# Delta stage: 16x16 diagonal blocks of a triangular inverse taken through DRAM to VectorE, decays from loaded rows, keys four steps ahead

## The chip, the cores and the metric

One core of a Trainium2 chip runs the whole program once. The metric is the device time of that execution in microseconds; the median of three runs stands for a kernel. All data is float32.

## The reference, cut to what matters

The model has two blocks of two layers each over 512 tokens (two streams of 256) of width 1024. The change lies in one mixer of the second block, a delta rule with 8 key heads, 16 value heads, head size 128, in both directions. For one chunk of 128 tokens, one value head, one direction:

```
g      = cumulative sum of the log decays over the chunk
A[i,j] = beta[i] * exp(g[i]-g[j]) * (k[i].k[j])      for j < i, else 0
N      = (I + A)^-1                                  unit triangular, 128 x 128
R      = v - exp(g) * (k @ S)                        S: state ahead of the chunk
new    = N @ R, scaled by beta
out    = exp(g) * (q @ S) + (q.k * exp(g[i]-g[j]), j <= i) @ new
S      = exp(g_last) * S + (k * exp(g_last-g)).T @ new
```

N, the inverse of a unit triangular matrix, is what the change computes in another way. A triangular inverse can be built by doubling: with the inverses of two neighbouring diagonal blocks of size s known, the block between them is minus one inverse times the block of A times the other. Seven levels (s = 1, 2, 4, ... 64) give a 128 x 128 inverse.

## The kernel before, in words

All engines run programs written out by hand, with semaphores between them; nothing is scheduled by a tool. The delta stage (pe_delta, act_delta, pool_delta, dve_delta, sp_delta) has 16 problems: problem x = 4 i + c is chunk c of the head group i, and it holds 4 value heads in both directions, which are interleaved (number 2n of a row is direction 0, 2n+1 direction 1) so that one inverse serves both. Problem s updates the state in step s, and the loops run over s from -2 to 15. In step s each engine works on three problems, in an order that the loop body writes out: the state, new values and output of problem s; levels 3 to 6 of the inverse of a = s+1; the decays, keys and levels 1 and 2 of n = s+2. Level 0 is done on VectorE in dve_first.

A level is the same chain each time. ScalarE copies blocks of the inverse (act_mixed, line 1841), TensorE turns them (pe_turn, line 1569), ScalarE copies the result out of PSUM (act_turned, line 1847). Meanwhile TensorE multiplies A by the inverse so far (pe_left, line 1560) and VectorE masks that (dve_left, line 2093). Then TensorE multiplies both (pe_right, line 1578), and VectorE subtracts the product from the inverse (dve_right, line 2101). All of these work on four heads, 128 x 512 numbers.

The decays of problem n come from GpSimd (pool_gates, line 1906), a product with a triangular matrix on TensorE (pe_decays, line 1521), one exponential (act_decays, line 1825) and a mask on GpSimd (pool_masks, line 1926). The keys are products on TensorE (lines 1538 and 1539), multiplied by beta and the decays in dve_keys (lines 2109, 2113, 2118) and turned (pe_turn_keys, line 1547). The state part is pe_state_keys (1589), dve_state_in (2142), pe_new_values (1616), act_tails (1856), act_new_values (1868), pe_queries (1628), pe_out (1639), pe_state_next (1647), dve_state_next (2168) and dve_out (2155).

SP, the queue of the weight stream, writes a small table of decays to DRAM once (line 1688), and in a step with c > 0 loads two rows of it into all partitions (line 1700); pool_queries (line 1937) multiplies them by the queries. Ahead of the stage the projections run (line 230, with the convolution on VectorE at line 1953), behind it the z products (line 230 again). A wait blocks everything that stands behind it on its engine.

## Time and profile before

| | us |
|---|---|
| runs | 3119.36, 3128.99, 3128.74 |
| median | 3128.74 |
| span of the profiled execution (first to last instruction) | 3124.0 |
| busy: TensorE, weight loads, VectorE, ScalarE, GpSimd | 2994.7, 2337.4, 1396.2, 714.2, 623.6 |
| delta stage: first decay product, first z product after it | 1539.83, 1999.40 |

The profile is of one execution; its own time is not listed beside the runs, so its span of 3124.0 us is set beside their median. PE is TensorE, PEld its weight loads, DVE VectorE, ACT ScalarE, POOL GpSimd, SP SyncE; a q behind a name is that engine's queue of instructions. The granted clock 1.00 is 2.4 GHz, 0.50 is 1.2 GHz.

### The profile page before, as it was taken

To read this page: it belongs to the slowest core of one execution; us is meant where nothing else is said; L and a number is where in the kernel's file an instruction comes from. 1 tells how busy PE (TensorE), PEld (TensorE's weight loads), DVE (VectorE), ACT (ScalarE), POOL (GpSimd) and SP (SyncE) were. 2 spreads that over 40 slices of the span, in tenths; PEclk is the share of its full clock that TensorE was granted. 3 is DMA by queue.
4 is the path that set the end of the run, shared out by engine and by line. 5 is a ranking of instruction groups with operands and counts; after the bars stand their busy time and mean duration, and the time that the engine had idled before them with its cause. 6 is when DMAs were issued, how large, how long until landed. Compare 5 with 4: busy or idle time off the path is not lost.

```text
span 3124.0 us, 39229 instructions
## 1 busy us (share of the span) xinstructions
PE 2994.7 (96%) x15545; PEld 2337.4 (75%) x15545; DVE 1396.2 (45%) x2271; ACT 714.2 (23%) x1336; POOL 623.6 (20%) x497
## 2 busy tenths in 40 slices
PE   7999999999999999999889999989999999999999
PEld 3565488887666888544488988878688887698888
DVE  2245478753244332455456666575454222223100
ACT  1134121100332330333244444321100001321100
POOL 1000145443000000000122322244355441020000
PEclk9999999999999999999999999999999999999999
DMA  7446222223436444433100000222122223111443
GB/s 295 173 158 243 94 82 94 81 95 104 133 128 227 164 148 148 188 135 148 62 8 13 16 15 15 82 80 81 68 90 86 84 92 125 69 41 54 148 148 108
DMA packets 51952, 337.66 MB, mean 108 GB/s; under 512 B 6448, under 2 KB 8112, under 8 KB 12752
## 3 DMA queue, kind: packets, MB, share of 16 engines
q1 hardware_dynamic: 47088, 323.05, 28.5%
q10 hardware_dynamic: 3120, 7.14, 0.6%
q0 software_dynamic: 1584, 5.21, 0.5%
q8 instruction: 116, 1.90, 0.2%
q14 instruction: 44, 0.36, 0.0%
HBM read 334.26 MB, written 1.11 MB: 107 GB/s over the span
## 4 chain that ended last, share of the span: by engine, by line
PE 82%; issue 10%; DVE 3%; ACT 2%; DVEq 1%; DMA 1%; POOL 0%; POOLq 0%; ACTq 0%; SPq 0%
PE psum L2694 28%; PE psum L230 21%; PE psum L355 3%; PE psum L1578 3%; PE psum L264 3%; PE psum L660 3%; PE psum L1560 3%; PE psum L2250 2%; PE psum L1569 1%; PE psum L490 1%; PE psum L517 1%; ACT h_sb L1045 1%; PE psum L1616 1%; PE psum L1521 1%; PE psum L1639 1%
## 5 line engine op out<-in xcount | busy, mean ns | idle before, releaser
L230 PE MATMUL psum<-h_sb,ring 128*128 128x256 f32 (+1 forms) x2400 | 728.6, 464 | 18.7 <-ACT h_sb L1045 18.7
L230 PEld LDWEIGHTS psum<-h_sb,ring 128*128 128x128 f32 x2400 | 456.2, 192 | 278.9 <-issue 223.5
L2694 PE MATMUL psum<-arena,ring 128*128 128x256 f32 x1688 | 383.2, 379 | 0.2 <-DVE arena L2757 0.2
L2694 PEld LDWEIGHTS psum<-arena,ring 128*128 128x128 f32 x1688 | 320.6, 190 | 44.2 <-DVE arena L2757 0.6
L2694 PE MATMUL psum<-arena,c 128*128 128x256 f32 x1080 | 249.0, 379 | 0.0
L230 PE MATMUL psum<-arena,ring 128*128 128x256 f32 x992 | 220.9, 386 | 9.4 <-DVE arena L1015 4.7
L2694 PEld LDWEIGHTS psum<-arena,c 128*128 128x128 f32 x1080 | 205.1, 190 | 29.7 <-issue 1.9
L1906 POOL TENSOR_TENSOR ring<-c,gates 128x512 f32<-128x512 f32 x32 | 32.6, 1041 | 950.9 <-PE psum L264 735.0
L230 PEld LDWEIGHTS psum<-arena,ring 128*128 128x128 f32 x992 | 192.5, 194 | 37.8 <-DVE arena L1015 5.1
L2694 PE MATMUL psum<-h_sb,ring 128*128 128x256 f32 x688 | 155.7, 379 | 8.6 <-DVE kst L2773 8.6
L2709 POOL TENSOR_TENSOR rows<-ring 128x512 f32<-128x512 f32 (+1 forms) x39 | 52.9, 1356 | 553.1 <-DVE arena L2737 334.7
L2723 ACT COPY kst<-psum 128x256 f32<-128x256 f32 x55 | 20.3, 369 | 612.9 <-PE psum L2694 583.9
L2694 PEld LDWEIGHTS psum<-h_sb,ring 128*128 128x128 f32 x688 | 130.5, 190 | 28.6 <-issue 11.1
L1953 DVE SCALAR_TENSOR_TENSOR arena<-psum,vec,arena 128x508 f32<-128x508 f32 (+1 forms) x128 | 95.6, 748 | 113.6 <-ACT arena L1712 106.1
L472 DVE SCALAR_TENSOR_TENSOR x_sb<-psum,mods,x_sb 128x256 f32<-128x256 f32 x48 | 22.5, 482 | 239.5 <-PE psum L230 190.0
L355 PE MATMUL psum<-ring,h_sb 128*128 128x256 f32 x512 | 117.5, 389 | 10.4 <-ACT h_sb L1045 10.4
L264 PE MATMUL psum<-ring,silu_w 128*32 128x256 f32 x1536 | 107.9, 410 | 18.4 <-DMA ring<-in_stream 11.6
L2711 POOL TENSOR_TENSOR ring<-ring 128x512 f32<-128x512 f32 (+1 forms) x79 | 122.3, 1548 | 14.6 <-issue 4.0
L355 PEld LDWEIGHTS psum<-ring,h_sb 128*128 128x128 f32 x512 | 97.4, 193 | 31.9 <-issue 11.7
L2713 POOL TENSOR_TENSOR c<-ring 128x512 f32<-128x512 f32 (+1 forms) x79 | 113.0, 1430 | 11.2
L1560 PE MATMUL psum<-ring 128*128 128x128 f32 x768 | 105.3, 278 | 7.3 <-DVE ring L2101 6.6
L264 PEld LDWEIGHTS psum<-ring,silu_w 128*32 128x32 f32 x1536 | 43.5, 115 | 89.8 <-issue 47.4
(321 smaller groups left out, 4388.7 us busy)
## 6 DMA issues: line engine op xcount, KB each, us to landing
ring<-in_stream SPq DMA_DIRECT2D x302, 1024.0 KB, 4.8
arena<-decays SPq DMA_DIRECT2D x24, 256.0 KB, 3.6
x_sb<-in_x ACTq DMA_DIRECT2D x1, 2048.0 KB, 19.1
arena<-in_rpb POOLq DMA_DIRECT2D x32, 64.0 KB, 8.1
arena<-in_c POOLq DMA_DIRECT2D x1, 1120.0 KB, 9.7
x_sb<-in_ctx ACTq DMA_DIRECT2D x1, 1024.0 KB, 10.0
c<-in_c ACTq DMA_DIRECT2D x1, 1024.0 KB, 4.9
out<-x_sb POOLq DMA_DIRECT2D x1, 1024.0 KB, 5.0
```

The lines of the kernel that those rows point to most:

```text
L230: ins = pe.matmul(out_ap, lhs(k), rhs(k), start=first and k == 0, stop=last and k == nk - 1)
L264: ins = pe.matmul(bank(7)[32 * j:32 * (j + 1), 0:256], silu[:, a // (2 * ADA_CHUNKS), k, ADA_ROWS - 2 - 2 * q:2 * ADA_ROWS - 2 - 2 * q], w ...
L355: ins = pe.matmul(bank(rho % 4)[:, tt * 256:(tt + 1) * 256], h[:, k, tok:tok + 128], w[:, slot, k, :], start=k == 0, stop=k == KT - 1)
L660: ins = pe.matmul(bank(rho % 4)[:, 0:tok], w[:, n % RING, k, rho % 2 * 128:(rho % 2 + 1) * 128], y[:, k, 0:tok], start=first and k == ks[0 ...
L1560: ins = pe.matmul(self.part(self.b["bank"](2 * p), n), self.part(self.M[p], n), self.mixed(self.DT[x % 3], level, 1, n), start=True, stop= ...
L1578: ins = pe.matmul(self.part(self.b["bank"](2 * p + 1), n), self.part(self.LT[p], n), self.part(self.Y[p], n), start=True, stop=True)
L1953: ins = dve.scalar_tensor_tensor(z[:, :, lo:hi], u[:, :, lo + shift:hi + shift], b["v"]("dn_conv", 1, 20 * j + 5 * q + 2 + shift), z[:, :, ...
L2250: ins = pe.matmul(bank(rho % 2)[:, tt * 256:(tt + 1) * 256], h[:, k, tok:tok + 128], w[:, (n0 + c) % RING, k, :], start=k == 0, stop=k == ...
L2694: ins = pe.matmul(dst, self.seven_weights(n, i, k, nk), self.seven_moving(x, sums, i, k, nk), start=first and j == 0 and k == 0, stop=last ...
L2709: pool.tensor_tensor(s3, a11, a21, ALU.subtract)
L2711: pool.tensor_tensor(a21, a21, a22, ALU.add)
L2713: pool.tensor_tensor(s2, a21, a11, ALU.subtract)
```

## The change

- Levels 0 to 3 are no longer doubled over 128 x 128 tiles. The matrix A (negated, so that dve_right adds) of each problem is written to DRAM in two lanes: as it stands and turned. From there the 16 x 16 blocks on the diagonal are loaded so that one partition holds one block (32 blocks a lane and problem, two problems in 128 partitions). VectorE inverts all of them at once in the free dimension: dve_inverse_fours, dve_inverse_eights, dve_inverse_last, in every even step for the two problems s+2 and s+3. The inverses go to DRAM and come back as rows (E), and GpSimd writes them as diagonal blocks into the inverse (pool_inverse). Levels 4, 5 and 6 stay as they were, for one problem at a time, with one set of buffers.
- The decays: rows of the cumulative sums are loaded into all partitions (sum_rows), GpSimd adds a mask of 0 and -1e30 (pool_bars), and ScalarE takes eight exponentials of 128 columns with the negated sum as bias (act_decays). The products with a triangular matrix, their gates and masks are gone.
- Keys and decays are made for n = s+4 instead of s+2; the loops begin at -4. The decay tiles have five buffers, A four.
- The order on all engines is written anew, and SP's program with it.

The core of the diff:

```diff
+BASE = 16
+LEVEL0 = 4
+LEV = LEVELS - LEVEL0
+LEAD = 4
+KEYS_PITCH = 128 // BASE * (BASE * 128 + BASE)
...
+        for hv in range(12, DN_HEADS):
+            self.pe_turn_v(pe, hv)
+        for s in range(-LEAD, DELTA_STEPS):
             if s == 0:
                 pe.wait_ge(T["v_copied"], DN_HEADS)
                 pe.wait_ge(S["mods_ready"], 5)
...
+            a, n = self.problem(s + 1), self.problem(s + LEAD)
             c = s % 4 if s >= 0 else None
...
             if c is not None and c > 0:
                 self.pe_state_keys(pe, s, 0)
             if a is not None:
...
+                self.pe_left(pe, a, 4)
             if c is not None and c > 0:
                 self.pe_state_keys(pe, s, 1)
             if a is not None:
...
+                self.pe_turn(pe, a, 4)
+            if c is not None:
+                self.pe_key_turn(pe, s)
             if n is not None:
                 self.pe_keys(pe, n, 0)
+            if a is not None:
+                self.pe_right(pe, a, 4)
             if c is not None:
...
+                self.pe_new_values(pe, s)
             if a is not None:
...
+                self.pe_left(pe, a, 5)
+            if c is not None and c > 0:
+                self.pe_queries(pe, s, 0)
+            if a is not None:
+                self.pe_turn(pe, a, 5)
+            if c is not None and c > 0:
+                self.pe_queries(pe, s, 1)
             if n is not None:
                 self.pe_keys(pe, n, 1)
             if a is not None:
...
+                self.pe_right(pe, a, 5)
             if c is not None:
...
+                self.pe_out(pe, s, 0)
             if a is not None:
...
+                self.pe_left(pe, a, 6)
+            if c is not None:
+                self.pe_out(pe, s, 1)
             if n is not None:
                 self.pe_turn_keys(pe, n)
...
             if a is not None:
                 self.pe_turn(pe, a, 6)
             if c is not None and c < 3:
                 self.pe_state_next(pe, s, 0)
             if a is not None:
                 self.pe_right(pe, a, 6)
...
             if c is not None and c < 3:
                 self.pe_state_next(pe, s, 1)
...
+        T = self.S2
+        rows, sums = self.b["decays"], self.b["gsums"]
+        keys_d, inv_d = self.b["keys_d"], self.b["inv_d"]
+        def row_of(dram, s, d):
+            i, c = divmod(s, 4)
+            at = 32 * ORDER[d][c] + 16 * d + 4 * i
+            return bass.AP(tensor=dram.tensor, offset=128 * at, ap=[[0, 128], [1, 512]])
+        def sum_rows(x):
+            for d in range(2):
+                sp.dma_start(self.AT[x % 5][d], row_of(sums, x, d)).then_inc(T[f"rows{x % 5}"], 16)
+        def keys_out(x, lane, tile):
+            dst = bass.AP(tensor=keys_d.tensor, offset=(2 * x + lane) * 4 * KEYS_PITCH,
+                          ap=[[128, 128], [KEYS_PITCH, 4], [1, 128]])
+            sp.dma_start(dst, self.heads(tile)).then_inc(T["keys_out"], 16)
+        def own_blocks(x, lane):
+            src = bass.AP(tensor=keys_d.tensor, offset=(2 * x + lane) * 4 * KEYS_PITCH,
+                          ap=[[BASE * 128 + BASE, 32], [128, BASE], [1, BASE]])
+            at = 64 * lane + 32 * (x % 2)
+            dst = self.inv[at:at + 32, :].rearrange("p (r i) -> p r i", r=BASE)
+            sp.dma_start(dst, src).then_inc(T["blocks"], 16)
         sp.wait_ge(T["decays_out"], 1)
...
+        sp.dma_start(rows, self.decay_rows).then_inc(T["decays_out"], 16)
+        sp.dma_start(sums, self.gsum_rows).then_inc(T["decays_out"], 16)
+        sp.wait_ge(T["decays_out"], 33)
         sp.wait_ge(T["qkv_ready"], QKV_CHUNKS // 2 + 1)
...
+        sp.wait_ge(self.b["S"]["products"], 2 * self.b["sched"]["2z"][0])
+        for x in range(5):
+            sum_rows(x)
+        for s in range(-LEAD, DELTA_STEPS):
+            n = self.problem(s + LEAD)
+            if s > 0:
+                for d in range(2):
                     sp.wait_ge(T[f"op{d}"], s)
...
+                if n is not None:
+                    sum_rows(n)
+                if s % 4 > 0:
+                    for d in range(2):
+                        sp.dma_start(self.QE[d], row_of(rows, s, d)).then_inc(T["qd"], 16)
+            m = self.batch(s)
+            if m is not None:
+                sp.wait_ge(T["inv"], m + 1)
+                for lane, tile in enumerate((self.inv, self.inv_turned)):
+                    dst = bass.AP(tensor=inv_d.tensor, offset=(128 * m + 32 * lane) * 256, ap=[[64 * 256, 2], [256, 32], [1, 256]])
+                    sp.dma_start(dst, tile[64 * lane:64 * lane + 64, :]).then_inc(T["inv_out"], 16)
+                sp.wait_ge(T["inv_out"], 32 * (m + 1))
+                for x in (2 * m, 2 * m + 1):
+                    if x > 1:
+                        sp.wait_ge(T["id"], x - 1)
+                    src = bass.AP(tensor=inv_d.tensor, offset=(128 * m + 64 * (x % 2)) * 256, ap=[[BASE, 128], [8 * 256, 8], [1, BASE]])
+                    if x % 2:
+                        sp.wait_ge(T["inv_in"], 16 * x)
+                    sp.dma_start(self.E[x % 2].rearrange("p (h i) -> p h i", h=8), src).then_inc(T["inv_in"], 16)
+            if n is not None:
+                sp.wait_ge(T["kr"], 2 * n + 2)
+                keys_out(n, 0, self.LTK)
+                sp.wait_ge(T["keys_out"], 32 * n + 16)
+                own_blocks(n, 0)
+                sp.wait_ge(T["mc"], n + 1)
+                keys_out(n, 1, self.M[n % 4])
+                sp.wait_ge(T["keys_out"], 32 * (n + 1))
+                own_blocks(n, 1)
+    def batch(self, s):
+        return s // 2 + 1 if s % 2 == 0 and -2 <= s < DELTA_STEPS - 2 else None
...
+        for hv in range(12, DN_HEADS):
+            self.act_turned_v(act, hv)
+        for s in range(-LEAD, DELTA_STEPS):
+            a, n = self.problem(s + 1), self.problem(s + LEAD)
             c = s % 4 if s >= 0 else None
...
             if a is not None:
                 self.act_mixed(act, a, 4)
+                self.act_turned(act, a, 4)
+            if n is not None:
+                self.act_decays(act, n, 0)
             if c is not None:
                 self.act_tails(act, s)
...
+                self.act_new_values(act, s, 0)
             if a is not None:
                 self.act_mixed(act, a, 5)
+            if c is not None:
+                self.act_new_values(act, s, 1)
+            if n is not None:
+                self.act_decays(act, n, 1)
+            if a is not None:
+                self.act_turned(act, a, 5)
+                self.act_mixed(act, a, 6)
+            if c is not None and c % 2 == 0:
+                self.act_out(act, s)
             if n is not None:
                 self.act_turned_keys(act, n)
             if a is not None:
...
                 self.act_turned(act, a, 6)
...
+    def act_decays(self, act, x, d):
+        T = self.S2
+        i, c = divmod(x, 4)
+        act.wait_ge(T["barred"], 2 * x + d + 1)
+        for n in range(4):
+            hv = 16 * d + 4 * i + n
+            part = self.part(self.AT[x % 5][d], n)
+            ins = act.activation(part, part, ACT.Exp, bias=self.ngcum[:, ORDER[d][c], hv:hv + 1])
+        ins.then_inc(T["ec"], 1)
     def act_turned_keys(self, act, x):
...
+        T = self.S2
         act.wait_ge(T["mt"], x + 1)
...
+        if x >= 4:
+            act.wait_ge(T["yp"], LEV * (x - 3))
+            act.wait_ge(T["keys_out"], 32 * (x - 3))
+        act.copy(self.M[x % 4], self.b["bank"](2)).then_inc(T["mc"], 1)
...
     def pool_delta(self, pool):
...
+        for s in range(-LEAD, DELTA_STEPS):
+            n, m = self.problem(s + LEAD), self.problem(s + 2)
             if n is not None:
...
+                self.pool_bars(pool, n)
+            if s > 0 and s % 4 > 0:
+                self.pool_queries(pool, s)
             if m is not None:
...
+                self.pool_inverse(pool, m)
+    def pool_bars(self, pool, x):
+        T, spread = self.S2, self.b["spread"]
+        pool.wait_ge(T[f"rows{x % 5}"], 32 * (x // 5 + 1))
         for d in range(2):
...
+            sums = self.heads(self.AT[x % 5][d])
+            pool.tensor_tensor(sums, sums, spread(self.bar(d), 4, 1), ALU.add).then_inc(T["barred"], 1)
+    def pool_inverse(self, pool, x):
+        T, spread = self.S2, self.b["spread"]
+        pool.wait_ge(T["inv_in"], 16 * (x + 1))
+        if x > 2:
+            for d in range(2):
+                pool.wait_ge(T[f"vn{d}"], x - 2)
+        own = spread(spread(self.own_block, 4, 1), BASE, 3)
+        dst = self.DT[x % 3].rearrange("p (h b i d) -> p h b i d", h=4, b=8, d=2)
+        src = self.E[x % 2].rearrange("p (d h i) -> p d h i", d=2, h=4)
         for d in range(2):
...
+            ins = pool.tensor_tensor(dst[:, :, :, :, d], spread(src[:, d], 8, 2), own, ALU.mult)
+        ins.then_inc(T["id"], 1)
...
+        for s in range(-LEAD, DELTA_STEPS):
+            if s == 0:
...
                 dve.wait_ge(T["v_copied"], DN_HEADS)
...
+            a, n, m = self.problem(s + 1), self.problem(s + LEAD), self.batch(s)
             c = s % 4 if s >= 0 else None
+            if c is not None and c > 0:
+                self.dve_state_in(dve, s, 0)
             if a is not None:
...
+                self.dve_left(dve, a, 4)
             if c is not None and c > 0:
...
+                self.dve_state_in(dve, s, 1)
             if a is not None:
...
+                self.dve_right(dve, a, 4)
+            if m is not None:
+                self.dve_inverse_fours(dve, m)
             if n is not None:
                 self.dve_keys(dve, n, 0)
             if a is not None:
...
+                self.dve_left(dve, a, 5)
+            if m is not None:
+                self.dve_inverse_eights(dve)
             if a is not None:
...
                 self.dve_right(dve, a, 5)
...
+            if m is not None:
+                self.dve_inverse_last(dve)
             if a is not None:
                 self.dve_left(dve, a, 6)
             if n is not None:
...
+                self.dve_keys(dve, n, 1)
             if c is not None and c < 3:
                 self.dve_state_next(dve, s, 0)
             if a is not None:
                 self.dve_right(dve, a, 6)
...
             if c is not None and c < 3:
                 self.dve_state_next(dve, s, 1)
...
+            if c is not None and c % 2:
+                self.dve_out(dve, s)
...
     def dve_keys(self, dve, x, d):
...
+        T = self.S2
         i, c = divmod(x, 4)
...
+        src, decays = self.b["bank"](2 + d), self.AT[x % 5][d]
+        dve.wait_ge(T["ec"], 2 * x + d + 1)
+        dve.tensor_copy(self.tail[x % 5][d], self.heads(decays)[:, :, LAST[d]])
         dve.wait_ge(T["kk"], 2 * x + d + 1)
+        if d == 0 and x > 0:
+            dve.wait_ge(T["mt"], x)
+            dve.wait_ge(T["keys_out"], 32 * x - 16)
         for n in range(4):
             hv = 16 * d + 4 * i + n
...
+            dve.scalar_tensor_tensor(self.part(self.LTK if d == 0 else self.tmp, n), self.part(src, n // 2),
+                                     self.nbeta[:, ORDER[d][c], hv:hv + 1], self.part(decays, n), ALU.mult, ALU.mult)
         dve.drain()
+        if d == 1:
+            dve.tensor_tensor(self.LTK, self.LTK, self.tmp, ALU.add)
         at = decays.rearrange("p (k r c) -> p k r c", k=2, r=2)
         kq = src[:, 256:512].rearrange("p (k c) -> p k c", k=2)
...
+        dve.tensor_tensor(at, at, self.b["spread"](kq, 2, 2), ALU.mult).then_inc(T["kr"], 1)
...
+    def dve_inverse_fours(self, dve, m):
+        T = self.S2
+        dve.wait_ge(T["blocks"], 64 * (m + 1))
+        if m > 0:
+            dve.wait_ge(T["inv_out"], 32 * m)
+        dve.tensor_tensor(self.inv, self.inv, self.c2[:, CD["upper"]:CD["upper"] + BASE * BASE], ALU.mult)
         dve.drain()
...
+        dve.memset(self.inv_at(0, (BASE + 1, BASE)), 1.0)
+        for at, row, col, shape in ((2, (1, (68, 4), (0, 2)), (18, (68, 4), (1, 2)), ((68, 4), (1, 2))),
+                                    (3, (2, (68, 4), (16, 2)), (35, (68, 4), (0, 2)), ((68, 4), (16, 2)))):
+            new = self.half[:, 0:8].rearrange("p (q c) -> p q c", q=4)
+            dve.tensor_tensor(new, self.inv_at(*row), self.inv_at(*col), ALU.mult)
+            dve.drain()
+            dst = self.inv_at(at, *shape)
+            dve.tensor_tensor(dst, dst, new, ALU.add)
+            dve.drain()
+    def dve_inverse_pairs(self, dve, size, tops):
+        n, cells = len(tops), size * size
+        wide = self.tmp[:, 0:n * cells * size].rearrange("p (a k) -> p a k", k=size)
+        half = self.half[:, 0:n * cells]
+        for side in range(2):
+            for q, top in enumerate(tops):
+                corner = top + size
+                out = wide[:, q * cells:(q + 1) * cells, :].rearrange("p (a b) k -> p a b k", a=size)
+                if side == 0:
+                    rows = self.inv_at(top, (BASE, size), (0, size), (1, size))
+                    cols = self.inv_at(corner, (0, size), (1, size), (BASE, size))
+                else:
+                    rows = self.b["spread"](half[:, q * cells:(q + 1) * cells].rearrange("p (a k) -> p a k", a=size), size, 2)
+                    cols = self.inv_at(top + size * (BASE + 1), (0, size), (1, size), (BASE, size))
+                dve.tensor_tensor(out, rows, cols, ALU.mult)
+            dve.drain()
+            if side == 0:
+                dve.tensor_reduce(half, wide, AX.X, ALU.add)
+            else:
+                for q, top in enumerate(tops):
+                    out = wide[:, q * cells:(q + 1) * cells, :].rearrange("p (a b) k -> p a b k", a=size)
+                    dve.tensor_reduce(self.inv_at(top + size, (BASE, size), (1, size)), out, AX.X, ALU.add)
+            dve.drain()
+    def dve_inverse_eights(self, dve):
+        self.dve_inverse_pairs(dve, 4, (0, 8 * (BASE + 1)))
+    def dve_inverse_last(self, dve):
+        self.dve_inverse_pairs(dve, 8, (0,))
+        turned = self.inv_turned[64:128, :].rearrange("p (r c) -> p r c", r=BASE)
+        dve.tensor_copy(turned, self.inv[64:128, :].rearrange("p (c r) -> p r c", r=BASE))
+        dve.drain().then_inc(self.S2["inv"], 1)
```

In the small functions of the levels (pe_left, pe_turn, pe_right, act_mixed, act_turned, dve_left, dve_right) only the buffers and the counts that they wait for change; dve_right adds instead of subtracting. pe_keys waits for kr of the problem before, and the end of the stage on SP waits for vn in place of yp1. inv_at makes a view of the inverse tile, (stride, count) pairs behind an offset.

## Rows read from the trace of the kernel before

**Rows 1.** The page, part 1: busy time and share of each engine.
```profile
PE 2994.7 (96%) x15545; PEld 2337.4 (75%) x15545; DVE 1396.2 (45%) x2271; ACT 714.2 (23%) x1336; POOL 623.6 (20%) x497
```
**Rows 2.** Chain that ended last, delta stage: start us, us, what; decays of two steps.
```profile
1616.96 1.72 PE psum L1521 x4
...
1942.43 1.72 PE psum L1521 x4
```
**Rows 3.** Busy time by stretches: length, then each engine, clock, DMA share, GB/s.
```profile
1700.00:1750.00 50.00, 47.90 (x400) 45.72 (x399) 31.52 (x68) 25.41 (x61) 14.15 (x16) 1.00 0.12 22
```
**Rows 4.** Timeline, weight loads of one step: start us, us, engine, line, operation.
```profile
1749.23 0.98 PEld L1560 LDWEIGHTS psum<-ring 128*128 128x128 f32 x8
...
1750.14 0.47 PEld L1569 LDWEIGHTS psum<-ident,kst 128*128 128x128 f32 x4
...
1750.58 0.97 PEld L1647 LDWEIGHTS psum<-arena 128*128 128x128 f32 x8
```
**Rows 5.** Instructions by line, 1600 to 1980: count, busy us, mean ns, idle before.
```profile
L2101 DVE TENSOR_TENSOR ring<-ring,psum 128x512 f32<-128x512 f32 x84 | 57.6, 686 | 73.7 <-PE psum L1578 73.7
L2113 DVE SCALAR_TENSOR_TENSOR ring<-psum,gates,ring 128x128 f32<-128x128 f32 x106 | 29.8, 344 | 1.4
...
L1841 ACT COPY kst<-ring 128x512 f32<-128x512 f32 x84 | 55.7, 663 | 36.2 <-DVE ring L2101 36.2
L1847 ACT COPY kst<-psum 128x512 f32<-128x512 f32 x85 | 50.0, 588 | 89.9 <-PE psum L1569 88.8
L1868 ACT ACTIVATE arena<-psum,gates 128x128 f32<-128x128 f32 x117 | 32.0, 386 | 5.0 <-PE psum L1616 5.0
...
L1906 POOL TENSOR_TENSOR ring<-c,gates 128x512 f32<-128x512 f32 x26 | 26.5, 1042 | 202.6 <-PE psum L1560 202.6
L1926 POOL TENSOR_TENSOR ring<-rinv,c 128x512 f32<-128x512 f32 x14 | 17.6, 1274 | 25.2 <-ACT rinv L1825 25.2
```
**Rows 6.** Timeline, two small VectorE operations with a drain between.
```profile
1564.78 0.17 DVE L1065 TENSOR_SCALAR amul<-mods 128x16 f32<-128x16 f32 x1
...
1565.03 0.18 DVE L1067 TENSOR_TENSOR amul<-amul,vec 128x16 f32<-128x16 f32 x1
```
**Rows 7.** DMAs: line 1700's landings, an issue, stretches, and issues of part 6.
```profile
DMA to landing us min/median/max: 3.0/3.6/5.5
...
1769.45 1.21 SPq L1700 DMA_DIRECT2D arena<-decays  x2
...
1770.00:1770.50 0.50, 0.50 (x7) 0.50 (x7) 0.00 (x0) 0.19 (x2) 0.00 (x0) 1.00 0.09 33
...
1773.00:1773.50 0.50, 0.50 (x6) 0.48 (x5) 0.00 (x0) 0.50 (x2) 0.00 (x0) 1.00 0.57 131
...
x_sb<-in_ctx ACTq DMA_DIRECT2D x1, 1024.0 KB, 10.0
...
decays<-gates SPq DMA_DIRECT2D x1, 64.0 KB, 6.2
```
**Rows 8.** Timeline at the start of the stage.
```profile
1545.40 0.80 SPq L1700 DMA_DIRECT2D arena<-decays  x2
1546.45 1.21 DVE L2109 COPY small<-ring 128x4 f32<-128x4 f32 x1 [1.15 <-POOL ring L1926]
```
**Rows 9.** Timeline and one stretch: levels with nothing beside them, and the clock.
```profile
1554.69 2.08 PE L1560 MATMUL psum<-ring 128*128 128x128 f32 x8 [0.68 <-ACT ring L1831]
...
1555.00:1556.00 1.00, 1.00 (x6) 1.00 (x6) 0.00 (x0) 0.19 (x1) 0.00 (x0) 0.50 0.00 0
...
1558.39 1.13 PE L1578 MATMUL psum<-rows,kst 128*128 128x128 f32 x8 [0.77 <-ACT kst L1847]
...
1562.68 1.13 PE L1578 MATMUL psum<-rows,kst 128*128 128x128 f32 x8 [0.77 <-ACT kst L1847]
```
**Rows 10.** Timeline at the end of the stage.
```profile
1989.16 1.13 PE L1578 MATMUL psum<-rinv,kst 128*128 128x128 f32 x8
...
1999.40 13.90 PE L230 MATMUL psum<-h_sb,ring 128*128 128x512 f32 x32
```

393 lines of the change are left out of this document (117 added, 276 removed).

## The prediction

> **What bounds the kernel now.** The page first: TensorE is busy for 96% of the span [rows 1]. The chain that ended last says where the changed stage lies: each step has the decay matmuls of line 1521 once, from 1616.96 to 1942.43 thirteen times, so a step takes 27.1 us [rows 2]. The busy time by stretches says what limits it: TensorE 48 us in 50, with VectorE at 32, ScalarE at 25, GpSimd at 14 [rows 3]. In the timeline a product of four heads takes TensorE 0.91 us, a turn of four heads 0.44 [rows 4]. So a full step is 12 products of levels (10.9), 6 turns (2.6), the decays (1.72), and twelve products and two turns for keys and state (11.8), near 27 in all: TensorE is the bound, and nothing waits on a DMA inside a step.
>
> **What goes.** Levels 1 to 3 leave TensorE: 3 x (2 x 0.91 + 0.44) = 6.8 us a step, and the decay matmuls 1.7. VectorE loses 6 passes of 0.69 and the three of dve_first, 2.1; ScalarE loses 3 x (0.66 + 0.59) [rows 2, 4, 5]. TensorE's own work falls from 27 to some 18.5 us a step. Were that the bound still, 14 steps would give back 120 us. The question is what chain takes its place.
>
> **What comes on VectorE.** By size, from rows: 512 numbers a partition 0.69 us, 16 numbers 0.18, and 0.08 between two operations with a drain between them [rows 5, 6]. No row sums along an axis at these sizes; I take the time of a product over as many numbers (ends: half and twice that, 2 us a batch either way). 256 numbers I put at 0.42, between the two. A batch for two problems: dve_inverse_fours 0.42, a memset 0.1, four operations of 8 numbers 0.16 each, drains, 1.7; dve_inverse_eights, four products of 64 numbers and three sums, 1.8; dve_inverse_last, two products of 512, two sums, one copy of 256, 3.6. That is 7.1 us in every even step. dve_keys for lane 1 adds the lanes, 512 numbers, as dve_first did: 0.2 for the tail (four numbers), 4 x 0.28, 0.69, 0.69 and a drain, 2.8 [rows 5]; lane 0 is 2.1. VectorE stays near 16 us a step: beside other work, except where it stands in a chain.
>
> **What comes on the other engines.** ScalarE's one exponential of 512 numbers, near 0.6, becomes 8 of 128, 0.27 each, 2.2 [rows 5]. GpSimd's two gates and two masks (1.04 and 1.27 each, 4.6 us) become two additions of 1.04 and two block writes of 1.27: equal, but the additions now wait for a DMA.
>
> **The DMAs.** Where there was one pair of loads a step, there are two pairs, two writes and two loads more, and in even steps four more, all on SP's queue. No row shows a write of 256 KB in pieces of 512 bytes, nor a load in pieces of 64. Nearest are loads of 256 KB: 3.0 us at least, 3.6 in the middle. A pair, issued at 1769.45, has its first data in the half microsecond from 1770.0 and its last in that from 1773.0: 4.1 us. A 64 KB write took 6.2, but behind 2 MB of the stream; 1 MB in 1024 pieces took 10.0, also behind the stream [rows 7]. I take 3.0 for each write or load (the bound nearest to an empty queue), 2.8 for the two writes of 64 KB, 0.5 for an issue, 4.4 for the pair of rows behind a load. The low end is 2.2, an estimate: 0.9 to the first data, 0.8 for the pieces, 0.5 after them. The high end is 5, half of what 1024 pieces took. By the Trainium skill's page "DMA: Bandwidth & Descriptors" (Anatomy of one DMA, measured for GpSimd's queue) a DMA costs 2.0 us plus its bytes at 436 GB/s, most of the 2.0 until the write is confirmed; for 256 KB that is an estimate of 2.6, and with it for every lane written the forecast would be some 9 us lower.
>
> **The new chain.** In a step SP waits for kr of problem n = s + 4, and only then writes lane 0, waits, loads blocks, writes lane 1, waits, loads blocks. Only after that does it reach sum_rows of the next step. Those rows are used in that same step, and act_decays of lane 0 stands on ScalarE ahead of the tails, the new values and level 5. From kr of one step (time K) to kr of the next:
> - lane 0 written 3.0, issue 0.5, lane 1 written 3.0, issue 0.5, rows 4.4: 11.4
> - pool_bars, lane 0: 1.05; act_decays, lane 0: 1.1
> - ScalarE in its order: tails 2.2, new values 1.1, mixed 5 0.7, new values 1.1, decays of lane 1 1.1, turned 5 0.6: 6.8
> - right 5 on TensorE 1.2 and VectorE 0.7, left 6 the same: 3.8
> - dve_keys, lane 1: 2.8
>
> Sum 26.9 us. The same walk without the DMAs, from right 6 to right 6: right 6 itself 1.9, level 4's copy, turn and state products up to turned 4 3.9, then 1.1, 6.8, 3.8 and 2.8 as above, and turn_keys, its copy and turned 6 2.0: 22.3. So the DMAs, and not an engine, set an odd step. An even step has dve_inverse_last between right 5 and left 6 (3.6), and SP must first write the inverses (2.8), load E (3.0), and wait for that before it issues the second E (0.5): 6.3 after the batch, where kr comes 3.5 after it (left 6 0.7, keys 2.8). That adds 2.8, so 33.3. Moved past on the queues: QE's pair stands behind the rows (queries end some 5 us after pool_bars, before turn 5, so hidden), and turn_keys stands ahead of turn 6: 2.4 from kr to right 6.
>
> **The start.** SP can load rows only from 1545.40, when the last projection is done. Before, the first keys began at 1546.45, since their decays need no load [rows 8]. Now: rows 4.5, bar 1.05, exponentials 1.1, keys 4.9: kr of problem 0 at 1557. Problem 1 is 7.3 later; its blocks land at 1573.5; fours, keys, eights, last: 1582.7; inverses out and in, GpSimd 2.5: 1591. Levels 4, 5, 6 take 4.3 us each when nothing covers them (right product 1558.39 to the next 1562.68 [rows 9]), with problem 3's keys between them 15: right 6 of problem 0 at 1606. Step 0 has its rows already. Its batch ends 17.3 later (right 6 1.9, level 4's copies and turn 2.0, exponentials 1.1, ScalarE 6.8, right 5 1.9, last 3.6), and SP is free for the keys 6.3 after that: 1629.6.
>
> **The sum.** Steps 1 to 11: six of 26.9 and five of 33.3, 328 us: 1957.5. Step 12 starts 2.4 later, at 1960. Without exponentials of new keys its batch ends after 15.1, and the inverse is in place after 8.4 more (2.8, 3.0, GpSimd 2.5), at 1983.5, which holds up step 13. From there to right 6 it is 11.3 (17.3 less 1.9, 1.1, 1.1 and 3.6, with 1.7 for level 6's copies), step 14 is 13.4, and the last step stays 10.2 (1989.16 to 1999.40 [rows 10]): 2018.4. Before, the z products start at 1999.4. That is 19 slower. TensorE now has holes of 3 us and more twice a step. After such a hole (1545 to 1553) the granted clock was still 0.50, the 1.2 GHz level, at 1555, and a product of four heads took 2.08 instead of 1.13 [rows 9]. I charge one group a step: 12 us. Together 31: the profiled execution's span of 3124.0 becomes 3155. That span is 4.7 below 3128.74, the median of the runs; with the same 4.7 around it the time is 3160.
>
> **Rivals.**
> - The DMAs are hidden, so that the steps are those of the walk without them: 22.3, and 25.9 with a batch. Step 1 at 1629, eleven steps 263, then 56: the z products at 1948, 51 earlier: 3078. Against it: it needs the 11.4 us of trips done in 5, and 0.9 passes from an issue to its first data alone [rows 7]. Chance 0.10.
> - Short trips, 2.2 us each, and no loss of clock: 43 trips in the loop (22 lane writes, 11 pairs of rows, 10 of the batches) x 0.8 = 34 us less, 3 at the start: 3111, faster than before. The price is smaller packets and an empty queue; it decides below 2.5 us a trip. Chance 0.18.
> - Small pieces are dear: 5 us for a write in 512 pieces and 10 for E in 1024, as 1024 pieces took 10.0 [rows 7]. Each step +4, each even one +7 more, the start +15: 3255. For it: nothing moves in pieces of 64 bytes now. Against it: that row stood behind other loads. Chance 0.15. The Trainium skill's page "DMA: Bandwidth & Descriptors", Specifications, says that pieces under 512 bytes are read, changed and written back; it gives no time for it, and no run here shows it yet.
> - That the change leaves out less than it says, say the levels on TensorE, cannot be: the loops over levels 1 to 3 are gone from the diff.
>
> Forecast 0.57, of which 0.11 falls within 0.3% of the old median (about what a measurement of this kernel can tell from no change), and 0.46 above.
>
> **Numbers.** Faster: 0.10 and most of 0.18: 0.27. Within 0.3%: 0.11. Slower: 0.46 and 0.15, rounded 0.62. The range leaves out the hidden case (0.10) and half of the dear one: 3095 to 3215; an error of 2 us a step moves the time by 24.
>
> **What would show it.** Line by line: GpSimd's additions idle for DMA rows in nearly every step; SP waits for kr and for its own writes; steps of alternating length, about 27 and 33; TensorE some 60% busy in the stage, with the clock at 0.50 in places; a write landing near 3.0. Wrong if GpSimd waits for TensorE instead of DMA, if steps have one length near 22, or if the stage ends before 1999.

## The result, and the profile after

The changed kernel takes 3182.73 us (median of 4 runs, 3176.41 to 3183.51), the kernel before 3124.05 us beside it (4 runs, 3118.47 to 3128.99): ratio 1.0179, 95% interval 1.0158 to 1.02. The change makes the kernel 1.8% slower. Forecast were 3160 and 3095 to 3215. The profiled execution took 3183.51 us, its span is 3181.3.

The page of the changed kernel, parts 1 and 4 and one row of part 5 (GpSimd's additions to the rows):

```profile
PE 2923.3 (92%) x14521; PEld 2276.7 (72%) x14521; DVE 1375.7 (43%) x2289; ACT 685.4 (22%) x1352; POOL 613.8 (19%) x481
...
PE 72%; issue 10%; DMA 6%; DVE 5%; ACT 4%; DVEq 1%; POOL 1%; SPq 1%; POOLq 0%; ACTq 0%
...
L1923 POOL TENSOR_TENSOR ring<-ring,c 128x512 f32<-128x512 f32 x32 | 40.7, 1294 | 928.0 <-DMA ring<-gsums 907.1
```

TensorE lost 71 us of work [rows 1], and the time rose by 59. The second line says where it went: 6% of the chain that ended last are now DMAs. The busy time by stretches, for the stretch of [rows 3]:

```profile
1700.00:1750.00 50.00, 36.34 (x243) 34.81 (x244) 23.53 (x61) 19.28 (x58) 11.82 (x12) 0.81 0.25 60
```

TensorE is busy for 36 us where it was 48, at a granted clock of 0.81 where it was 1.00. No engine is full: a chain sets the time. Here it is, from the kr of step 1 (the signal by which VectorE says that the keys of a problem are ready, here of problem 5) to the rows of step 3 (chain of waits in order of time: start, us, what):

```profile
1669.85 2.28 DMA keys_d<-kst
...
1672.90 2.34 DMA keys_d<-silu_w
...
1675.68 0.42 SPq L1669
...
1676.15 4.98 DMA ring<-gsums
...
1681.19 1.28 POOL ring L1923
...
1683.78 2.06 ACT arena L1883 x8
1685.84 1.03 ACT arena L1894 x4
...
1691.49 0.91 PE psum L1551 x8
...
1696.75 0.37 DVE vec L2189
...
1697.73 4.67 DMA inv_d<-vec
1702.42 2.29 DMA c<-inv_d
...
1705.19 2.50 DMA keys_d<-kst
...
1708.08 2.46 DMA keys_d<-c
...
1711.45 4.17 DMA ring<-gsums
```

Not all pieces are shown. It is the loop of the forecast: both key writes, the rows, GpSimd, ScalarE's tails and new values, right 5, VectorE's last part of the inverse, then the inverses out and in, and the keys again. The turning of the keys on TensorE (line 1521, right behind kr) gives its period, from the timeline:

```profile
1637.96 1.11 PE L1521 MATMUL psum<-ident,kst 128*128 128x128 f32 x4 [5.22 <-DVE ring L2131]
...
1669.88 0.72 PE L1521 MATMUL psum<-ident,kst 128*128 128x128 f32 x4 [2.36 <-DVE ring L2131]
1700.45 1.11 PE L1521 MATMUL psum<-ident,kst 128*128 128x128 f32 x4 [5.22 <-DVE ring L2131]
1731.91 1.12 PE L1521 MATMUL psum<-ident,kst 128*128 128x128 f32 x4 [2.36 <-DVE ring L2131]
...
1951.88 1.11 PE L1521 MATMUL psum<-ident,kst 128*128 128x128 f32 x4 [5.22 <-DVE ring L2131]
```

Ten steps from 1637.96 to 1951.88 took 313.9 us, 62.8 a pair; forecast were 60.2, before it was 54.2 [rows 2]. The z products behind the stage start later by 58.5 us than in [rows 10], which is the whole loss:

```profile
2057.94 13.90 PE L233 MATMUL psum<-h_sb,ring 128*128 128x512 f32 x32
```

### The profile page after: what moved, and what is told of

Read it like the earlier page. It is cut to its first block, busy times and chain, and to the rows that moved or that the text cites. A ratio compares the mean times of both kernels' runs of the same rounds, so it can differ in the third digit from the quotient of the medians.

```text
span 3181.3 us, 37412 instructions
## 1 busy us (share of the span) xinstructions
PE 2923.3 (92%) x14521; PEld 2276.7 (72%) x14521; DVE 1375.7 (43%) x2289; ACT 685.4 (22%) x1352; POOL 613.8 (19%) x481
## 3 DMA queue, kind: packets, MB, share of 16 engines
q1 hardware_dynamic: 103328, 343.04, 30.5%
## 4 chain that ended last, share of the span: by engine, by line
PE 72%; issue 10%; DMA 6%; DVE 5%; ACT 4%; DVEq 1%; POOL 1%; SPq 1%; POOLq 0%; ACTq 0%
PE psum L2751 28%; PE psum L233 21%; PE psum L358 3%; PE psum L267 3%; PE psum L663 3%; PE psum L2307 2%; DMA ring<-gsums 2%; PE psum L493 1%; DMA inv_d<-vec 1%; PE psum L520 1%; DMA ring<-in_stream 1%; ACT h_sb L1048 1%; PE psum L1551 1%; PE psum L2408 1%; DMA keys_d<-kst 1%
## 5 line engine op out<-in xcount | busy, mean ns | idle before, releaser
L2751 PEld LDWEIGHTS psum<-arena,c 128*128 128x128 f32 x1080 | 205.1, 190 | 29.7 <-issue 1.9
L1923 POOL TENSOR_TENSOR ring<-ring,c 128x512 f32<-128x512 f32 x32 | 40.7, 1294 | 928.0 <-DMA ring<-gsums 907.1
L358 PEld LDWEIGHTS psum<-ring,h_sb 128*128 128x128 f32 x512 | 97.5, 193 | 31.8 <-issue 11.7
L2770 POOL TENSOR_TENSOR c<-ring 128x512 f32<-128x512 f32 (+1 forms) x79 | 113.1, 1432 | 11.2
L2766 POOL TENSOR_TENSOR c<-ring 128x512 f32<-128x512 f32 (+1 forms) x40 | 53.1, 1327 | 262.6 <-PE psum L2751 236.0
```

Source lines behind the costliest of these rows:

```text
L358: ins = pe.matmul(bank(rho % 4)[:, tt * 256:(tt + 1) * 256], h[:, k, tok:tok + 128], w[:, slot, k, :], start=k == 0, stop=k == KT - 1)
L1923: pool.tensor_tensor(sums, sums, spread(self.bar(d), 4, 1), ALU.add).then_inc(T["barred"], 1)
L2751: ins = pe.matmul(dst, self.seven_weights(n, i, k, nk), self.seven_moving(x, sums, i, k, nk), start=first and j == 0 and k == 0, stop=last ...
L2766: pool.tensor_tensor(s3, a11, a21, ALU.subtract)
L2770: pool.tensor_tensor(s2, a21, a11, ALU.subtract)
```

## The experiments

Each kernel ran beside the kernel before on the same chip; its median there was 3128.08 us for the first four, 3126.88 for the next four, 3125.94 for the next two and 3128.26 for the last. Where a text says how far a kernel lies under the changed one, it compares medians with 3182.73, which was run beside 3124.05. By the intervals of the ratios, a difference between two kernels holds to some 8 us where both have about ten runs, and to some 10 to 13 where one has only four or five. The theory: SP's queue is on the path, because rows needed in a step are asked for only after the keys of the step before have made their trips. The rivals: VectorE's inverting, or the throttled clock, is what costs.

**Rows earlier.** Same loads, same data; SP asks for the rows of step s+1 in step s, behind the output products, ahead of its wait for the inverses' writes and of the keys.

```diff
             n = self.problem(s + LEAD)
-            if s > 0:
-                for d in range(2):
-                    sp.wait_ge(T[f"op{d}"], s)
-                if n is not None:
-                    sum_rows(n)
...
                     sp.dma_start(dst, tile[64 * lane:64 * lane + 64, :]).then_inc(T["inv_out"], 16)
+            if 0 <= s < DELTA_STEPS - 1:
+                for d in range(2):
+                    sp.wait_ge(T[f"op{d}"], s + 1)
+                if self.problem(s + LEAD + 1) is not None:
+                    sum_rows(s + LEAD + 1)
...
+            if m is not None:
                 sp.wait_ge(T["inv_out"], 32 * (m + 1))
```

> Rows of decays for the next step are asked for in this step, as soon as its output products are done, ahead of the waits for the inverses and the keys on SP. Theory A (the step is set by a loop over SP: keys written, keys written, rows loaded, exponentials, keys): the rows leave the loop, GpSimd's additions hardly wait for a DMA, steps 1 to 11 fall from 31 us on average to between 22 and 27, and the time falls by 50 to 80 us, to 3103 to 3133. Rival B (VectorE's added work and the lower clock set the step, the rows only wait in the shadow): less than 15 us gained, 3168 or more.

Measured: 3120.34 us (10 runs, 3107.34 to 3130.47), ratio 0.998 (0.996 to 1.0). Some 62 us came back by moving loads on a queue, with nothing taken from any engine. GpSimd's waits in the stage, grouped by line from 1600 to 1950, the changed kernel first:

```profile
L1923 POOL TENSOR_TENSOR ring<-ring,c 128x512 f32<-128x512 f32 x21 | 26.6, 1285 | 150.1 <-DMA ring<-gsums 129.1 <-PE psum L1589 21.0
L1936 POOL TENSOR_TENSOR ring<-c,small 128x512 f32<-128x512 f32 x10 | 10.4, 1057 | 118.1 <-DMA c<-inv_d 118.1
```

and with the rows earlier:

```profile
L1924 POOL TENSOR_TENSOR ring<-ring,c 128x512 f32<-128x512 f32 x22 | 27.7, 1280 | 64.7 <-DMA ring<-gsums 64.7
L1937 POOL TENSOR_TENSOR ring<-c,small 128x512 f32<-128x512 f32 x14 | 14.5, 1057 | 198.3 <-DMA c<-inv_d 198.3
```

The wait for rows is halved. What is late next is the inverse: its first load (L1937) now ends more idle time, and in the odd steps level 4 waits for it.

**One key write.** Leaves out the write of the turned lane; both lanes of blocks are read from the first, so the inverses of lane 1 are of other numbers.

```diff
-                sp.wait_ge(T["mc"], n + 1)
-                keys_out(n, 1, self.M[n % 4])
-                sp.wait_ge(T["keys_out"], 32 * (n + 1))
```

> Leaves out the second write of the keys (the turned lane; its blocks are read from the first lane's copy), so a step has one trip to DRAM less on SP. Theory A: each of steps 1 to 11 loses one trip and an issue, 2.7 to 2.9 us, the start loses two or three: 35 to 40 us less, 3143 to 3148. Rival B: the trip is in the shadow of the engines, at most 5 us less.

Measured: 3150.39 us (5 runs), ratio 1.008 (1.0051 to 1.011), 32 us under the changed kernel: 2.0 us for each of the 16 writes left out, where one took 2.3 in the chain above. The trips are paid nearly one for one.

**The inverses in four writes.** 32 partitions and one run of DRAM each, in place of two writes over 64 partitions whose destination has an outermost count of 2.

```diff
-                    dst = bass.AP(tensor=inv_d.tensor, offset=(128 * m + 32 * lane) * 256, ap=[[64 * 256, 2], [256, 32], [1, 256]])
-                    sp.dma_start(dst, tile[64 * lane:64 * lane + 64, :]).then_inc(T["inv_out"], 16)
+                    for q in range(2):
+                        dst = bass.AP(tensor=inv_d.tensor, offset=(128 * m + 64 * q + 32 * lane) * 256, ap=[[256, 32], [1, 256]])
+                        at = 64 * lane + 32 * q
+                        sp.dma_start(dst, tile[at:at + 32, :]).then_inc(T["inv_out"], 16)
```

> The inverses (128 KB a batch) are written by four DMAs of 32 partitions, whose outermost count is 32, instead of two whose outermost count in DRAM is 2. In the trace of the changed kernel those two take 5.2 us from the first issue to the end of the wait, against 2.3 for a 256 KB write. Theory A1 (they take long because their shape puts them on few DMA engines, and the trip is in SP's loop): the trip falls to 3 us in spite of one more us of issues, 2 us in each of 8 batches, 10 to 18 us less in all, 3165 to 3173. Rival (a fixed cost of small writes to DRAM): the trip stays near 5, the time within 4 us.

Measured: 3169.76 us (4 runs), ratio 1.0125 (1.0091 to 1.0158), 13 us under the changed kernel. The timeline of SP's queue, the changed kernel first, then this one:

```profile
1697.18 0.51 SPq L1706 DMA_DIRECT2D inv_d<-blk  x1
1697.73 0.48 SPq L1706 DMA_DIRECT2D inv_d<-vec  x1
1702.42 0.37 SPq L1714 DMA_DIRECT2D c<-inv_d  x1
```

```profile
1693.73 0.80 SPq L1708 DMA_DIRECT2D inv_d<-blk  x2
1694.57 0.89 SPq L1708 DMA_DIRECT2D inv_d<-vec  x2
1696.61 0.38 SPq L1716 DMA_DIRECT2D c<-inv_d  x1
```

The trip is 2.9 us in place of 5.2; of these 2.3, 1.6 a batch came off the time. With four runs the 13 us are barely clear of the noise; the trip itself is read from the trace.

**Part of the arithmetic left out.** The products and sums of the eights and of the last size; fours and the copy stay, so the inverses are incomplete.

```diff
-        self.dve_inverse_pairs(dve, 4, (0, 8 * (BASE + 1)))
...
-        self.dve_inverse_pairs(dve, 8, (0,))
```

> Leaves out VectorE's products and sums of dve_inverse_eights and dve_inverse_last (5.6 us a batch), keeping the copy, the signals and all DMAs. Theory A: dve_inverse_last stands between right 5 and left 6 and ahead of the write of the inverses: 3.9 us less in each even step, more at the start, eights hidden behind ScalarE: 25 to 38 us less, 3145 to 3158. Rival (the batch runs while VectorE would wait anyway): under 8 us.

Measured: 3154.7 us (4 runs), ratio 1.0082 (1.0054 to 1.0111), 28 us less. That is 3.5 us in each of 8 batches: the last part, 3.7 us without its copy, pays nearly in full (it stands between right 5 and left 6), the eights don't.

**Both mends.** Rows earlier and four writes.

> The changed kernel with both mends: the row loads for the next step issued behind the output products (as in the run with the early rows) and the inverses written by four DMAs of 32 partitions each. Theory A (with the rows out of the way the odd steps still begin with a stall on the inverse's own trip, some 6 us in each of 7 pairs of steps, so that what the trip loses comes off the time one for one): the trip is 2.3 to 3 us shorter, 7 times 2.3 to 3 = 16 to 21 us, 3099 to 3107 us against 3120 with the early rows alone. Rival B (the two more issues stand ahead of the row loads on SP's queue and the loop goes over that queue again): under 8 us saved, 3113 to 3125.

Measured: 3114.97 us (10 runs), ratio 0.9954 (0.9937 to 0.9971). Only 5 us less than the early rows alone, which is within the noise: theory A missed, and rival B's number held, but not for its reason. SP's queue in the timeline:

```profile
1726.41 0.84 SPq L1669 DMA_DIRECT2D ring<-gsums  x2
1727.29 0.91 SPq L1708 DMA_DIRECT2D arena<-decays  x2
1728.30 0.39 SPq L1717 DMA_DIRECT2D c<-inv_d  x1
1733.69 0.37 SPq L1717 DMA_DIRECT2D gates<-inv_d  x1
```

The load of the first inverse was issued 3.7 us behind the writes' first issue (1724.59), but landed 5.4 us later, at 1733.69, where the same load took 2.3 in the chain above. What differs is the megabyte of rows issued just ahead of it.

**The batch in one piece.** On top of both mends, VectorE does fours, eights and last together, ahead of the keys.

> As the run with both mends, and VectorE inverts the whole batch in one piece ahead of the keys, in place of three pieces between its other work. The inverses are ready some 4 us earlier in the even step. Theory A (VectorE's order is now the path of the even step: some 5.9 us of inverting stand ahead of the keys and of level 5, of which about 3 lay in idle time before): the even step gets 3 to 6 us longer and the stall at the odd step 4 us shorter, so -1 to +2 us in each pair, 3095 to 3120. Rival B (only the stall counts): 7 times 4 = 28 us less, 3071 to 3080.

Measured: 3131.14 us (10 runs), ratio 0.9999 (0.9982 to 1.0015). Both numbers missed. B is refuted; A had the sign, but put the loss too low: the step with the batch grew from 27.3 to 31.6 us (new values at 1612.11 and 1643.69, in place of 1612.14 and 1639.45), and the next shrank by 2 or less. A start of the inverse 4 us earlier gains nothing when kr, behind it on VectorE, is as much later.

**The clock.** 16 matmuls whose result is overwritten unread, in TensorE's hole ahead of the turned keys.

```diff
                 self.pe_out(pe, s, 1)
+                if n is not None:
+                    for q in range(16):
+                        pe.matmul(self.part(b["bank"](4), q % 4), self.part(self.R[0], q % 4), self.part(self.R[0], q % 4),
+                                  start=True, stop=True)
```

> The changed kernel with 16 matmuls of 128x128 put into TensorE's hole between the second output products and the turning of the keys (steps 0 to 11; their result is overwritten unread; 2.1 us at the full clock, 3.8 at the half). Theory A (the half clock that follows the holes costs one group a step, about 1 us, as forecast): the granted clock of the stage goes from about 0.82 to over 0.9 and the time falls by 5 to 15 us, 3168 to 3178. Rival B (the hole is too short for the filling or the half clock stretches only what waits anyway): 3180 to 3190, and over 3190 if the fillers themselves come onto the path.

Measured: 3183.05 us (4 runs), ratio 1.0171 (1.0133 to 1.0208), against 1.0179: no difference that four runs can tell (they leave room for some 13 us either way). The fillers took 3.74 us, not the 2.1 I had put. They fitted the hole of 5.2 us in one step of a pair; in the other, of 2.4 us, the turned keys began 1.1 us behind kr (1662.52 to 1663.62 in this run). The clock rose from 0.81 to 0.89 over the stage (1640 to 1985 in the changed kernel, 1633 to 1978 here), most of all in this stretch:

```profile
1750.00:1800.00 50.00, 40.56 (x330) 39.51 (x330) 26.16 (x63) 14.36 (x38) 9.32 (x10) 0.93 0.24 62
```

0.93 in place of 0.81 and no time for it: rival B's number. But most steps have two half-clock stretches, and the fillers took away only one. What stands behind the turned keys ends in a wait of TensorE for GpSimd (1.95 to 5.20 us ahead of line 1600), so a faster clock there gives nothing. The other stretch lies behind that wait, from the queries and the turn of level 5 (line 1542) to right 5 (line 1551), and it is on the chain. In the changed kernel, at a granted clock of 0.58:

```profile
1687.46 1.11 PE L1542 MATMUL psum<-ident,kst 128*128 128x128 f32 x4 [0.93 <-ACT kst L1868]
...
1689.41 0.67 ACT L1874 COPY kst<-psum 128x512 f32<-128x512 f32 x1
...
1691.33 1.06 PE L1551 MATMUL psum<-rows,kst 128*128 128x128 f32 x8
```

and with the fillers, at 0.50:

```profile
1680.72 1.11 PE L1546 MATMUL psum<-ident,kst 128*128 128x128 f32 x4 [1.13 <-ACT kst L1872]
1681.63 1.92 PE L1604 MATMUL psum<-arena 128*128 128x128 f32 x8
```

ScalarE's copy (line 1874) is done at 1690.08, but TensorE reaches right 5 only 1.25 us later; in the kernel with the inverse first (below), where the same groups run at 1.00, it starts 0.15 us behind the copy (1693.35 to 1693.50). With the fillers the gap is 1.7 us (1683.34 to 1685.04). Over eleven steps the gaps beyond 0.15 us add up to 10.0 us in the changed kernel and 10.4 with the fillers; with the inverse first there are none. So the run shows no cost of the one stretch. It leaves the other as it was, with some 10 us.

**Both mends and the fillers.**

> Both mends and the 16 filling matmuls. In the kernel with early rows alone the hole ahead of the turned keys was 5.2 us in the even step and 2.4 in the odd one, and the sixth level's products behind it ran at half clock (1.9 in place of 1.1 us). Theory A (the clock is worth about 1 us a step there): 5 to 12 us under the run with both mends. Rival B (the filling fills the odd steps' hole to the brim and delays what follows): 0 to 12 us over it.

Measured: 3125.66 us (10 runs), ratio 0.9985 (0.9963 to 1.0007): 11 us over both mends alone, which is rival B's number. Its reason does not show: the steps of 2.4 us of hole are no longer than without fillers (20.4 to 22.7 us from new values to new values, against 20.8 to 23.1). It is the others that grew, those with the wait for the inverse: 29.1 to 31.0 us, against 27.3 to 29.7. Level 4's left product behind that wait, with both mends alone and then with the fillers:

```profile
1634.92 1.15 PE L1533 MATMUL psum<-ring,c 128*128 128x128 f32 x8 [0.94 <-POOL ring L1939]
```

```profile
1635.00 2.00 PE L1537 MATMUL psum<-ring,c 128*128 128x128 f32 x8 [3.25 <-POOL ring L1943]
```

The inverse comes at the same time, but TensorE, faster behind its fillers, has idled 3.25 us for it and not 0.94. What follows runs at a granted clock of 0.72 and not 1.00, and the new values stand 6.15 us behind (1641.15) and not 4.53 (1639.45). This stretch is on the chain, and there the lower clock costs 1.6 us; in the next pair it is 2.6.

**The inverse first.** Both mends, but in a step with a batch the rows are issued only behind the first inverse's load.

```diff
+            if m is None:
+                rows_ahead(s)
...
                     sp.dma_start(self.E[x % 2].rearrange("p (h i) -> p h i", h=8), src).then_inc(T["inv_in"], 16)
+                    if x % 2 == 0:
+                        rows_ahead(s)
```

> Both mends, with the row loads of a step that has a batch moved behind the load of the first inverse. With both mends as run before, the four writes took 2.9 us, but the first inverse's load, issued at 1728.30 right behind four row loads, landed only at 1733.69 (5.4 us; 2.3 to 3.0 elsewhere). Theory A (it shares the DMA engines with the rows, 1 MB ahead of it): it lands 2.4 to 3 us earlier, the odd steps begin that much sooner, 7 times 2.4 = 17 us off 3115, 3094 to 3103. Rival B (the load is slow for its own 16-byte... pieces, or the rows, now 3 us later, hold the next step's decays): 3110 to 3125.

Measured: 3097.18 us (4 runs, 3090.4 to 3102.28), ratio 0.991 (0.9881 to 0.9939): theory A, 18 us (by the intervals 8 to 28) from the order of five loads. It beats both kernels. SP's queue in the timeline:

```profile
1721.07 0.79 SPq L1710 DMA_DIRECT2D inv_d<-blk  x2
1721.90 0.89 SPq L1710 DMA_DIRECT2D inv_d<-vec  x2
1723.93 0.38 SPq L1721 DMA_DIRECT2D c<-inv_d  x1
1724.41 1.11 SPq L1669 DMA_DIRECT2D ring<-gsums  x2
1725.57 0.90 SPq L1691 DMA_DIRECT2D arena<-decays  x2
1726.56 0.38 SPq L1721 DMA_DIRECT2D gates<-inv_d  x1
```

The load lands in 2.6 us at most (1723.93 to 1726.56), which is when the second could be issued. In this kernel's chain from 1690 to 1745 no DMA stands any more.

**The same order with two writes**, as the changed kernel has them.

> The same order on SP's queue, but the inverses written by two DMAs as in the changed kernel (landing in 5.2 us where four took 2.9). The rows are then issued only after that. Theory A (the trip of the inverse sets the start of the odd steps, and its parts add up): 2.3 us in each of 7 pairs, 16 us more than the run with four writes, 3110 to 3120. Rival B (the other transfers have become the limit): within 5 us of that run.

Measured: 3109.16 us (9 runs), ratio 0.9946 (0.9928 to 0.9965): 12 us over the run with four, nearer to A's 16 than to B's 5, and just below A's range; the noise here is about 11 us, so the time alone speaks for A only weakly.

**Two writes, another layout.** The inverses lie by lane in DRAM, so that each 64 KB write has an outermost count of 64; each E then takes two loads of 32 KB.

```diff
-                    dst = bass.AP(tensor=inv_d.tensor, offset=(128 * m + 32 * lane) * 256, ap=[[64 * 256, 2], [256, 32], [1, 256]])
+                    dst = bass.AP(tensor=inv_d.tensor, offset=(128 * m + 64 * lane) * 256, ap=[[256, 64], [1, 256]])
```

> The order of SP's queue with the inverse first, two DMAs of 64 KB for the inverses as in the changed kernel, but laid out in DRAM by lane, so that each writes 64 pieces of 1 KB in one run (outermost count 64 in place of 2); each E is then loaded by two DMAs of 32 KB. Theory A (a transfer with an outermost count of 2 is spread over two of the sixteen DMA engines, as the busy share of 0.13 in that stretch says): the writes land in 2.5 to 3.2 us and not in 5.2, the load of E costs 0.4 us more for its second issue, and the time is that of the run with four writes, 3092 to 3104. Rival B (64 KB out of a tile and in pieces of 1 KB takes its 5 us whatever the layout, and four writes helped because each was half as large): the trip stays near 5 us, 3107 to 3118.

Measured: 3099.45 us (6 runs), ratio 0.9918 (0.9898 to 0.9937). Queue:

```profile
1727.57 0.46 SPq L1708 DMA_DIRECT2D inv_d<-blk  x1
1728.07 0.60 SPq L1708 DMA_DIRECT2D inv_d<-vec  x1
1730.14 1.22 SPq L1721 DMA_DIRECT2D c<-inv_d  x2
```

As many writes, as many bytes and pieces of the same size as in the changed kernel, and the trip is 2.6 us, not 5.2. The stretch in which only those writes moved, in the changed kernel and here (the last three columns are clock, DMA share and GB/s):

```profile
1699.00:1701.50 2.50, 1.04 (x5) 1.05 (x6) 1.33 (x3) 0.00 (x0) 0.00 (x0) 0.50 0.13 38
```

```profile
1728.60:1730.10 1.50, 0.00 (x0) 0.00 (x0) 1.43 (x5) 0.00 (x0) 0.00 (x0) 0.50 0.35 87
```

0.13 is the share of two engines of sixteen (2/16 = 0.125). The Trainium skill's page "DMA: Bandwidth & Descriptors" (Why a DMA increments its semaphore by 16 and not by 1) says that the number of engines is the largest up to 16 that divides the outermost counts of both sides; for a count of 2 that is two engines, and this trace agrees.

## Why the prediction was right, and what it mis-sized

**The mechanism** held: SP's queue sets the steps. The edit that only moves the row loads gave back 62 us, the left-out write 32, the shorter inverse trip 13. Two of the signs named for it missed: the steps did not alternate between 27 and 33 us, and TensorE was 73% busy in the stretch of [rows 3] (36.34 of 50 us), not 60%.

**The loop.** Its terms against the chain above: the two key writes with their issues took 5.8 us from 1669.85 to 1675.68 (forecast 7.0), the rows 5.5 until GpSimd (forecast 4.4), the addition 1.3 (1.05). These errors cancel. Two more do: right 5 waits 1.25 us for TensorE at half clock, and the left product of level 6, counted at 1.2, lies beside VectorE's last part. From kr to kr behind the odd step came 30.6 us, the forecast 26.9 with the inverse's last part 3.6, so 30.5. The term of the forecast that was mis-sized most clearly is the inverse trip: "write 2.8, E 3.0, issue .5" was taken from 64 KB as a write that lands like others. The write took 5.2 and E 2.3; behind kr that is 4.8 us (1700.40 to 1705.19) where the forecast had 2.8. And its cost falls in the other step of the pair than I wrote: SP is late for the keys of the even step, so the odd step's rows are late. So the periods are 30.6 and 31.5, not 33.3 and 26.9; the pair, 62 to 63, is 60.2 and the trip's 2, and the rest is spread.

**The sum.** The z products came at 2057.94, forecast were 2018.4 and 12 for the clock. The 39.5 us, of which the 12 should cover the clock's share, fall in three places. Up to the keys of step 0 it is 13.0 (SP writes them at 1642.57, forecast 1629.6): the first kr 2.7, right 6 of problem 0 at 1612.55 and not 1606, so 3.9 more, and the walk with the batch and its trip from there 6.4. In eleven steps it is 14.9 (to 1985.34, 342.8 in place of 328), of which the trip's 2.0 in five or six batches is 10 to 12. In the last steps it is 11.7: the forecast gave levels 4.3 us each when nothing covers them, from [rows 9], but here keys, state and queries of the same step stand between them: the right products of problem 14 and 15 are 5.2 to 6.1 us apart.

**The clock** was a term of 12 us, one group at half clock in each step. No run measured it as a whole. The traces bear the size out, as an estimate: in eleven steps of the changed kernel TensorE comes 10.0 us late to right 5, all told. With the trip's 10 to 12 that is more than the 14.9 us of these steps; terms counted too high take the rest back (the key writes, the left product of level 6). The forecast did not say behind which of its two holes the cost lies. It lies behind the wait for the queries, and not behind the hole ahead of the turned keys, which the fillers filled to no effect.

**The rivals.** "Short trips" had the key writes about right (2.3 us) and the rows wrong: a pair of rows took 4.7 to 5.5 from its first issue. "Small pieces are dear" did not come: blocks and E in pieces of 64 bytes landed in 1.9 and 2.2 us. "The DMAs are hidden" was refuted for this kernel, but its walk without DMAs, 22.3 and 25.9 us, is what the kernel with the inverse first does where no DMA is on the chain: its new values stand 21.8 and 25.7 us apart (1687.30, 1709.11, 1734.83), and over the stage 20.4 to 23.1 and 25.7 to 27.0.

**The arithmetic** of a batch was forecast at 7.1 us (fours 1.7, eights 1.8, last 3.6). In the kernel with early rows VectorE needs 1.4, 1.7 and 4.1, together 7.2. In the changed kernel the fours run beside GpSimd and take 4.7 (1681.29 to 1686.04), but into time that was idle. Only the last part was on the path, as forecast.

**By the skill.** From the Trainium skill's page "DMA: Bandwidth & Descriptors" (Anatomy of one DMA) a 256 KB write was an estimate of 2.6 us; in the chain above it took 2.3 to 2.5. What mattered more, the outermost counts, I had left out of the forecast; looking at them would have pointed at the inverse trip.

**Open.** In the best kernel a step with a batch is still 3 to 6 us longer than the one behind it. VectorE's last part of the inverse stands on its chain with 4.0 us (1717.01 to 1721.01), but no run leaves it out there. No run fills the hole ahead of the queries either, so what the clock costs there rests on the estimate above. What VectorE's slowdown beside GpSimd (below) costs in time was not tried on its own.

## What to carry to other kernels

A queue that issues in program order is an engine like the others: write down for each transfer who needs it when, and issue the one with the earliest need first. Here the order of the same loads moved the time by some 80 us, and with the inverses' writes mended the kernel went from 1.8% slower to 0.9% faster on the same arithmetic. And take the outermost count of each side of a small transfer as part of its price: two writes of 64 KB landed in 5.2 us with a count of 2, and in 2.6 with 64. And before filling a hole to raise the clock, see which stretch at half clock is on the chain.

## What the runs showed of the hardware that I had not expected

- **Transfers that share the engines.** A 64 KB load that lands in 2.3 us took 5.4 behind 1 MB of broadcast rows issued in the 2 us ahead of it, and 2.6 ahead of them.
- **Two-input operations of VectorE slow down beside GpSimd.** The groups by line of the changed kernel, and of the one with early rows, where GpSimd's additions no longer coincide with the inverting:

```profile
L2150 DVE TENSOR_TENSOR blk<-blk 128x8 f32<-128x8 f32 x12 | 7.0, 584 | 1.2 <-issue 0.3
```

```profile
L2151 DVE TENSOR_TENSOR blk<-blk 128x8 f32<-128x8 f32 x14 | 2.4, 168 | 1.4 <-issue 0.3
```

  A product of 8 numbers takes 0.17 us alone; in the changed kernel it took 0.58 on average, up to 1.15 beside GpSimd. A product of 256 numbers went from 0.42 to 0.63 on average, and a copy of four numbers, with one input, from 0.16 (1667.27) to 0.61 (1686.04). The Trainium skill's page "GPSIMD Engine Reference" (Specifications) says that GpSimd shares its ways into the memory with VectorE's instructions of two inputs there; the trace agrees, though only by coincidence in time.
- **A product of 512 numbers in a pattern of four dimensions** took 1.03 us (line 2171), the sum over the same numbers 0.69, as a plain product does [rows 5]. I had put both at 0.69.
- **A mean clock says little.** Raising it from 0.81 to 0.89 over the stage moved no time that four runs could tell, since the groups that it sped up ended in a wait of 2 to 5 us. With both mends the fillers raised it from 0.91 to 0.96, and the kernel got 11 us slower: the half clock had moved onto the chain.
